# A two-block model on one Trainium2 core: order of logs, operands and gate bounds in the recurrent stage

## The reference

```python
def hgrn2_mixer(h, w_in, lb, onorm_g, w_out):
    q, fl, i, g = jnp.split(h @ w_in, 4, axis=-1)
    f = lb + (1.0 - lb) * jax.nn.sigmoid(fl)        # lb: bounds of the gates, from two rows of logits
    k, logf = 1.0 - f, jnp.log(f)
    # per head of 128 features, in chunks of 64 tokens; b = cumsum(logf) inside a chunk
    q_dec, k_inv, k_state = silu(q) * exp(b), k * exp(-b), k * exp(b_last - b)
    # A = mask(q_dec @ k_inv^T); o = A @ i + q_dec @ state; state = exp(b_last) * state + k_state^T @ i
    o = o * rsqrt(mean(o * o) + eps) * onorm_g
    return (o * silu(g)) @ w_out
```

## Time and profile before

| | |
|---|---|
| median of 3 runs | 3540.16 us (3540.02 to 3541.07) |
| the profiled execution | 3542.3 us |
| its span, first to last instruction | 3540.5 us |
| mean granted TensorE clock | 0.978 |
| TensorE busy | 3365.4 us, 95% |
| VectorE busy | 1650.2 us, 47% |
| ScalarE busy | 1161.3 us, 33% |
| HBM | mean 173 GB/s |
| the recurrent stage | 2850 to 3156 us of the span |

### The profile page before, as it was taken

The page is one execution under the profiler, slowest core; times in us unless marked ns, Lnnn a source line. Parts: engine busy times, 40 slices in busy tenths (PEclk is TensorE's granted clock), DMA queues, the critical chain, the costliest instruction groups (busy, mean ns, idle before and its releaser), DMA issues. The chain is left out here.

```text
span 3540.5 us, 41807 instructions
## 1 busy us (share of the span) xinstructions
PE 3365.4 (95%) x17328; PEld 2410.8 (68%) x17328; DVE 1650.2 (47%) x2514; ACT 1161.3 (33%) x1804; POOL 96.0 (3%) x79
## 2 busy tenths in 40 slices
PE   8989998999989989998999989999999999899998
PEld 6668875444447767876444437776788878778887
DVE  4564542212135664552121125435766674576665
ACT  5543322010125553232101114444433353543333
POOL 0000000000001000000000000000000010010000
PEclk9999998999989999998999999999999999999999
DMA  5122247999963112245999982321222222122222
GB/s 185 42 60 75 75 172 301 426 427 427 427 243 116 46 48 72 75 160 219 427 427 427 427 339 66 101 89 38 96 95 96 95 84 72 60 72 96 95 97 71
DMA packets 274939, 616.64 MB, mean 174 GB/s; under 512 B 10864, under 2 KB 210320, under 8 KB 225600
## 3 DMA queue, kind: packets, MB, share of 16 engines
q1 hardware_dynamic: 274224, 613.65, 45.6%
q10 hardware_dynamic: 528, 0.32, 0.0%
HBM read 609.71 MB, written 4.23 MB: 173 GB/s over the span
## 5 line engine op out<-in xcount | busy, mean ns | idle before, releaser
L456 PE MATMUL bank<-h_hi,w_hi 128*128 128x512 f32 x1784 | 711.4, 399 | 13.9 <-DVE w_lo L207 11.5
L458 PE MATMUL bank<-h_hi,w_lo 128*128 128x512 f32 x1784 | 698.3, 391 | 0.0
L457 PE MATMUL bank<-h_lo,w_hi 128*128 128x512 f32 x1784 | 698.2, 391 | 0.0
L207 DVE TENSOR_TENSOR w_lo<-w_raw,w_hi 128x2048 fp32r<-128x2048 f32 (+2 forms) x209 | 424.0, 2029 | 215.9 <-ACT w_hi L199 213.5
L2336 PE MATMUL bank<-expert_w,gathered 128*64 128x512 f32 x2016 | 448.2, 600 | 11.2 <-DMA expert_w<-in_w_exp_up 11.1
L199 ACT ACTIVATE w_hi<-w_raw 128x2048 fp32r<-128x2048 f32 (+2 forms) x209 | 355.4, 1701 | 234.7 <-PE bank L458 202.9
L456 PEld LDWEIGHTS bank<-h_hi,w_hi 128*128 128x128 f32 x1784 | 337.1, 189 | 102.7 <-issue 18.1
L458 PEld LDWEIGHTS bank<-h_hi,w_lo 128*128 128x128 f32 x1784 | 336.5, 189 | 72.3
L457 PEld LDWEIGHTS bank<-h_lo,w_hi 128*128 128x128 f32 x1784 | 337.3, 189 | 69.7 <-issue 1.9
L2336 PEld LDWEIGHTS bank<-expert_w,gathered 128*64 128x64 f32 x2016 | 144.4, 138 | 296.8 <-issue 290.8
L2336 PE MATMUL bank<-expert_w,hidden_t 128*64 128x512 f32 x1024 | 226.3, 595 | 0.0
(11 more groups left out here) (436 smaller groups left out, 4798.4 us busy)
## 6 DMA issues: line engine op xcount, KB each, us to landing
expert_w<-in_w_exp_up SPq DMA_DIRECT2D x64, 2048.0 KB, 22.1
expert_w<-in_w_exp_down SPq DMA_DIRECT2D x64, 2048.0 KB, 25.0
expert_w<-in_w_exp_gate SPq DMA_DIRECT2D x62, 2048.0 KB, 23.0
w_raw<-in_ffn_w_up SPq DMA_DIRECT2D x44, 1024.0 KB, 4.9
w_raw<-in_w_branch_gate SPq DMA_DIRECT2D x64, 512.0 KB, 3.8
w_raw<-in_w_in SPq DMA_DIRECT2D x22, 1024.0 KB, 5.0
w_raw<-in_ffn_w_down SPq DMA_DIRECT2D x22, 1024.0 KB, 4.9
w_raw<-in_hgrn_w_in SPq DMA_DIRECT2D x16, 1024.0 KB, 5.1
```

Source lines behind the costliest of these rows:

```text
L207: dve.tensor_tensor(self.w_lo[n % 2][:, 0:e], self.raw[n % self.RAW][:, 0:e], self.w_hi[n % 2][:, 0:e].bitcast(F32), ALU.subtract).then_in ...
L456: pe.matmul(out, st[0], mv[0], start=(j == 0), stop=False)
L457: pe.matmul(out, st[0], mv[1], start=False, stop=False)
L458: last = pe.matmul(out, st[1], mv[0], start=False, stop=(j == len(g.steps) - 1))
```

## The change

Three reorderings; no instruction of the source is added or removed.

1. `act`: in slots 7, 17, 27, 37 `logs` comes before the step of the pair before (in 17, 27, 37 that is `roots`). Slot 7 has no such step.
2. `dve`: in slots 9, 19, 29, 39 `operands` comes before the step of the pair before (in 19, 29, 39 `take_low`). Slot 9 has no such step.
3. `bounds_act` and `bounds_dve` become `pre_act` and `pre_dve` of tile 1 in place of tile 0. On ScalarE they then follow tile 0's two Tanh and the `w_hi` of tile 2, on VectorE the `w_lo` of tile 2 and tile 0's two operations.

```diff
--- before.py
+++ after.py
@@ -2977,6 +2977,8 @@
 
     def act(self, act, slot):
         g, step = self.steps(slot)
+        if slot < 40 and slot % 10 == 7:
+            self.logs(act, slot // 10)
         if g is not None:
             if step < 2:
                 self.copy_k_state(act, 2 * g + step)
@@ -2987,13 +2989,13 @@
             elif step == 9:
                 for h in (2 * g, 2 * g + 1):
                     self.take_high(act, h)
-        if slot < 40 and slot % 10 == 7:
-            self.logs(act, slot // 10)
         if slot < 40 and slot % 10 == 8:
             self.exps(act, slot // 10)
 
     def dve(self, dve, slot):
         g, step = self.steps(slot)
+        if slot < 40 and slot % 10 == 9:
+            self.operands(dve, slot // 10)
         if g is not None:
             if step < 2:
                 self.mask(dve, 2 * g + step)
@@ -3007,8 +3009,6 @@
                     self.take_low(dve, h)
         if slot < 40 and slot % 10 == 7:
             self.sums(dve, slot // 10)
-        if slot < 40 and slot % 10 == 9:
-            self.operands(dve, slot // 10)
 
 
     def logs(self, act, g):
@@ -3230,7 +3230,7 @@
                 features_out(v, i * P, 256, tanh_to(r.gate[g % 2], g, i, gated), times_one_more(r.gate[g % 2], i)) for i in range(2)]))
         for g in range(4):
             tiles.append(k_part_tile(v, w_out, g, [(r.o_hi[:, 2 * g + b, :], r.o_lo[:, 2 * g + b, :]) for b in range(2)], r.lo_taken.ge(2 * g + 2)))
-        tiles[0].pre_act, tiles[0].pre_dve = bounds_act, bounds_dve
+        tiles[1].pre_act, tiles[1].pre_dve = bounds_act, bounds_dve
         dense = Dense(v, None, tiles, banks=v.ps[0:3], ring=v.ring, first_banks=v.ps[5:7])
         after = next_norm(v.h_plain, dense, range(len(dense.flat) - KT, len(dense.flat)))
         dense.run(side=r, lead=lead, tail=after, following=following)
```

## The result

| | before | changed |
|---|---|---|
| median of 5 runs, us | 3540.02 (3535.54 to 3541.07) | 3519.53 (3518.61 to 3523.07) |
| span of the profiled execution, us | 3540.5 | 3517.8 |
| mean granted TensorE clock | 0.978 | 0.982 |

The ratio is 0.9947 with a 95% interval of 0.9932 to 0.9961. Forecast were 3519.9 us and a range of 3515.5 to 3526.0.

The account below looks back on a forecast made before the run. TensorE, busy 95% of the span, was taken to lose time in waits for `w_lo` and `operands` and slow clock behind them; 5.0 + 6.0 + 4.9 + 4.4 = 20.3 us gave a median of 3519.9 us, range 3515.5 to 3526.0.

Parts of the forecast that it names:

- The start: Tile 2 at the stage's start: moving the bounds gives 3.8 wait + 2.3 clock - 0.9 new wait, taken as 5.0 us.
- Slot 17: Logs first: two of four table loads go, `w_hi` 1.40 us and `w_lo` 3.72 us sooner, TensorE's wait for `w_lo` gone.
- The margin of 0.03 us: Slot 17: `w_lo` done at 2959.56, TensorE's next product possible at 2959.65; wait claimed gone with 0.03 us to spare.
- Slots 20, 30 and 40: Starts of `inner` after the gates: gains of 6.0, 4.9 and 4.4 us, the last limited by the mask of head 6.
- 3.5 + 2.7 - 0.4: Parts of the 6.0 us gain to `inner` in slot 20: wait removed, clock regained, less a new wait.
- its old place less 3.72: Slot 40: the mask of head 6 was to move by 3.72 us only, with VectorE's chain, and hold the second `inner`.
- (a): Slots 17, 27, 37: table loads do not fall away; each turn gives 1.4 us less, 16.1 in all, 3524.1 us; 6%.
- (b): ScalarE: a single table set serves Ln and Exp in the new order; 22.4 us in all, 3517.8 us; 3%.
- (c): TensorE's clock falls at the short waits, costing 6.6 us; gain 13.7 us, 3526.5 us; 8%.
- (d): No gain: VectorE's chain binds and moving `sums` forward only exchanges waits; 3%.
- (e): Slower: low TensorE clock from `inner` in slots 20, 30 and 40 on, 10 groups at 2.7 us, 3547 us; 2%.
- the terms for the clock (2.3, 2.7 and 1.6): Slow-clock time regained behind removed waits: 2.3 us at the start, 2.7 after slot 17, 1.6 after slot 27.

Follow-up runs that it names:

- operands alone: Only the move of `operands` (change 2) made on the kernel before; 1.38 us off the stage, ratio to before 0.9991 (0.9982 to 1.0).
- filler products: Changed kernel plus 17 unused products in front of `inner` of head 6 in slot 40; stage 287.86 us against 286.26.
- mask first: Changed kernel with VectorE doing the mask of head 6 before the `w_lo` of tile 17 in slot 40; stage 285.30 us against 286.26.
- loads back: Changed kernel plus an unused Ln behind the roots' Exp in slots 17, 27, 37, restoring both saved table loads; stage 290.76 us against 286.26.
- operands before scale: Changed kernel with `operands` one slot sooner in every turn, in front of `scale`; stage 289.93 us against 286.26.
- operands in slot 38: Changed kernel with head 6's mask before tile 17's `w_lo`, and the last pair's `operands` in slot 38; stage 284.21 us, ratio to before 0.9938.
- bounds alone: Only the bounds moved to tile 1 (change 3) on the kernel before; 6.44 us off the stage, ratio to before 0.9986 (0.9977 to 0.9995).

## Why the prediction was right

**The start.** TensorE's tile 2 was to wait 0.7 us and its second group 0.9; measured 0.74 and 0.82. The order of the next stage was a true picture of the new order here. Gain to head 0: 5.0 taken, 4.91 measured, with the clock at 1.00 in the first value group as taken. The 2.3 us of clock in this term is one trace's: with the operands alone the same group lost 1.64.

**Slot 17.** `w_hi` was to start 1.40 us sooner: this stretch lies 58.80 - 53.89 + 1.58 = 6.49 us sooner in the changed trace than before, so 2956.74 - 1.40 - 6.49 = 2948.85; measured 2948.83. `w_lo` was to follow at 2950.78; measured 2950.84. No wait for it, as computed. The margin of 0.03 us did not matter, since the next wait is behind it.

**Slots 20, 30 and 40.** The first `inner` was expected with a wait of about 0.4 us, it was 0.25: the row counts from the end of the last product, 0.16 us behind the moment at which the next could have started, from which the working counted. `inner` itself was expected at 2965.60 - 6.49 = 2959.11 and began at 2959.17. The same 0.16 is missing where the prediction names the parts of this turn: 3.5 + 2.7 - 0.4 is 5.8, not 6.0; with 0.25 for the new wait the parts give the 6.0 that the difference of the two starts gave. Gains of the turns: 6.0, 4.9 and 4.4 taken; measured 62.65 - 56.68 = 5.97, 61.58 - 56.74 = 4.84, and to head 7 (61.58 + 6.07) - (56.74 + 6.71) = 4.20. The last is the term with the largest miss, 0.2 us: the mask of head 6 was done at 3079.20, 0.08 later than its old place less 3.72 and less the earlier gains, and `inner` began 0.16 behind it where 0.08 was taken. In slot 40 the long wait was to be 4.4 (4.3) with the clock falling, and the mask was to set the second `inner`. It does: the experiments with filler products and with the mask first show it from both sides.

**The rivals.** (a), loads that stay: two per turn are gone, and putting them back costs 4.5 us in all, near the 4.2 that the rival's working gave. That earlier `sums` gain also without fewer loads, as this rival has it, is what "loads back" shows. (b), one set for Ln and Exp: the changed trace has a load between them as the one before, 1.28 us each time. What the Trainium skill says of a common set (ScalarE: Activation LUTs, "Table sets: the hidden batching unit") is not borne out here. That load between Ln and Exp is why the new order saves loads, 1.5 us a turn; the rest of the gain does not hang on it. (c), a clock that falls at the short waits: 1.00 behind the waits of 0.7, 0.8 and 0.25 us; this is the stretch behind the first of 0.25:

```profile
2959.17:2966.00 6.83, 6.83 (x36) 5.85 (x37) 6.53 (x9) 1.09 (x2) 0.00 (x0) 1.00 0.05 10
```

The prediction called on short waits with clock 1.00 around them, but no row of it shows one; the trace before has them, 0.90 us before 3134.74 and 1.74 before 3138.11, both with 1.00 around them. (d) and (e) did not arise.

**What was right by less than it seems.** 3519.9 against 3519.53 us hides errors that cancel: 0.4 us too much in the stage, and 2.8 us outside it that the change has nothing to do with, taken back by the profiled execution's distance from the median. The stage's 20.3 against 19.9 is the fair comparison, and even that is closer than the method can promise: the terms for the clock (2.3, 2.7 and 1.6) were read from the very trace against which the gain is measured. With the first stretch, slot 20 and slot 40 as the traces of the single parts had them, 0.66 + 1.53 = 2.2 us less, the stage would have gained 17.7.

## What to carry to other kernels

Price a reordering on the engine that it touches by walking the chain to the next engine's wait and then to the wait behind that one: here each wait that was removed had another behind it (0.8 us at the start, 0.25 in slots 20 and 30, 4.3 and 1.0 in slot 40), and those set the gain. Count what a wait of TensorE costs with the slow stretch behind it, 5.2 to 6.2 us for 3.5 here, unless another wait behind it hides the slow stretch, as the mask's did in slot 40. Group activations of one kind across independent steps where the order is written by hand, and look which load stands in front of the critical copy: that one counts, the others may be covered.

## What the runs showed of the hardware

The length of TensorE's wait did not settle whether its clock fell. Behind waits of 1.4 us (loads put back) it stayed at 1.00:

```profile
2949.22:2954.90 5.68, 5.68 (x24) 4.42 (x24) 5.58 (x10) 5.68 (x9) 0.00 (x0) 1.00 0.63 185
```

Behind a wait of 2.55 us it fell in one version and stayed in another; the stretch behind that wait with operands before scale, and then the one with operands in slot 38:

```profile
3080.39:3083.29 2.90, 2.89 (x6) 1.78 (x6) 2.21 (x3) 2.21 (x2) 0.00 (x0) 0.50 0.00 0
```

```profile
3076.82:3079.22 2.40, 1.64 (x6) 1.05 (x7) 2.40 (x5) 2.21 (x2) 0.00 (x0) 1.00 0.00 0
```

Right in front of both TensorE did the same work, `inner` and a group of six products in 2.93 us at 1.00 between waits of 0.94 and 2.55 us; further back the first version has waits for the mask that the other lacks. And behind the same wait of 3.53 us a features group took 8.29 and 8.21 us in slot 20 of two traces (before, operands alone) and 7.18 to 7.21 in slot 30 of both and in both slots with the bounds alone, against 5.57 at the full clock. What decides between these was not tried. For a forecast it means that each such wait carries an uncertainty of about 1 us, and a wait of 2.5 us one of over 1.
